# A decoder step in split fp32: convolution taps dealt differently, third output tile's weights first, last tile in column blocks

## What is computed

```
x = x + W_out [ conv_group(h) ; GLA_group(h) ],   h = RMSNorm(x), one projection W_in
x = x + CrossAttn(RMSNorm(x), memory K/V)         4 heads, 256 memory tokens
x = x + W_down relu(W_up RMSNorm(x))^2            4096 hidden
y = RMSNorm(x) * final_g
```

## Time and profile before

| | |
|---|---|
| median of three runs | 1539.58 us (1538.15 to 1540.58) |
| profiled execution | 1538.49 us |
| its span in the trace | 1536.8 us, granted PE clock 0.982 |
| PE busy | 1469.4 us, 96% |
| DVE, ACT, POOL busy | 611.8, 452.6, 383.5 us |
| DMA | 113.99 MB, mean 74 GB/s |

### The profile page before, as it was taken

The page is one execution under the profiler, slowest core; times in us unless marked ns, Lnnn a source line. Parts: engine busy times, 40 slices in busy tenths (PEclk is TensorE's granted clock), DMA queues, the critical chain, the costliest instruction groups (busy, mean ns, idle before and its releaser), DMA issues.

```text
span 1536.8 us, 22391 instructions
## 1 busy us (share of the span) xinstructions
PE 1469.4 (96%) x9454; PEld 1429.3 (93%) x9454; DVE 611.8 (40%) x681; ACT 452.6 (29%) x606; POOL 383.5 (25%) x292
## 2 busy tenths in 40 slices
PE   5799998998989999999999999999999999999994
PEld 5799997998779999988999999999999999999994
DVE  4759989995442355552322211112011110121213
ACT  6532252348252343341232211122012220032211
POOL 5753231122402311101222222222222222122220
PEclk9999999999889999999999999999999999999997
DMA  8411151011132241176111111111111111111102
GB/s 302 139 63 49 43 54 42 28 41 45 57 138 106 88 172 42 42 268 221 54 42 54 43 55 41 41 54 42 55 41 41 53 42 55 41 41 54 42 27 110
DMA packets 45273, 113.99 MB, mean 74 GB/s; under 512 B 7688, under 2 KB 20248, under 8 KB 43808
## 3 DMA queue, kind: packets, MB, share of 16 engines
q1 hardware_dynamic: 43312, 104.19, 20.6%
q10 hardware_dynamic: 1904, 8.98, 1.4%
HBM read 100.85 MB, written 12.30 MB: 74 GB/s over the span
## 4 chain that ended last, share of the span: by engine, by line
PE 83%; DVE 6%; issue 5%; ACT 3%; POOL 3%; DMA 0%; ACTq 0%; DVEq 0%; SPq 0%; POOLq 0%
PE ps L1080 57%; PE ps L1181 11%; PE ps L1433 5%; DVE ps L1644 2%; PE ps L1467 2%; PE m L1151 1%; POOL w_split L570 1%; PE ps L1386 1%; PE m L1346 1%; PE ps L1194 1%; PE ps L1446 1%; ACT w_split L633 1%; DVE x_res L2052 1%; PE m L1099 1%; POOL a_op L586 1%
## 5 line engine op out<-in xcount | busy, mean ns | idle before, releaser
L570 POOL TENSOR_TENSOR w_split<-w_raw,w_split 128x512 fp32r<-128x512 f32 x234 | 325.2, 1410 | 1094.1 <-ACT w_split L633 1094.0
L1080 PE MATMUL ps<-a_op,w_split 128*128 128x344 f32 x3312 | 524.0, 320 | 4.6 <-POOL w_split L570 4.6
L1080 PEld LDWEIGHTS ps<-a_op,w_split 128*128 128x128 f32 x3312 | 522.7, 189 | 5.0 <-DVE x_res L1845 4.8
L1080 PE MATMUL ps<-b_op,w_split 128*128 128x344 f32 x2304 | 362.6, 319 | 0.0
L1080 PEld LDWEIGHTS ps<-b_op,w_split 128*128 128x128 f32 x2304 | 361.7, 188 | 0.2
L1181 PE MATMUL ps<-a_op,w_split 128*128 128x344 f32 x1440 | 233.4, 321 | 0.0
L1181 PEld LDWEIGHTS ps<-a_op,w_split 128*128 128x128 f32 x1440 | 226.6, 188 | 1.9 <-issue 1.4
L633 ACT ACTIVATE w_split<-w_raw 128x1024 fp32r<-128x1024 f32 x117 | 122.8, 1050 | 243.4 <-PE ps L1080 238.6
L1644 DVE SCALAR_TENSOR_TENSOR ps<-conv_in,par,ps 128x1024 f32<-128x1024 f32 x116 | 149.7, 1290 | 3.7
L2023 DVE SCALAR_TENSOR_TENSOR tmp<-ps,rstd 128x1032 f32<-128x1032 f32 x32 | 39.4, 1233 | 215.1 <-PE ps L1080 203.2
L2033 DVE TENSOR_TENSOR x_res<-x_res,ps 128x1032 f32 x24 | 29.5, 1230 | 230.8 <-PE ps L1080 230.8
(11 more groups left out here) (206 smaller groups left out, 1046.4 us busy)
## 6 DMA issues: line engine op xcount, KB each, us to landing
w_raw<-in_wt SPq DMA_DIRECT2D x117, 512.0 KB, 3.5
cache_b<-in_cache_v SPq DMA_DIRECT2D x8, 1024.0 KB, 12.1
x_in<-in_x ACTq DMA_DIRECT2D x4, 1032.0 KB, 10.8
x_spill<-x_res SPq DMA_DIRECT2D x8, 516.0 KB, 2.6
out_y<-x_res ACTq DMA_DIRECT2D x8, 516.0 KB, 3.0
w_more<-in_wt SPq DMA_DIRECT2D x8, 512.0 KB, 4.0
cache_a<-in_cache_k SPq DMA_DIRECT2D x2, 2048.0 KB, 11.6
cache_b<-in_cache_k SPq DMA_DIRECT2D x2, 2048.0 KB, 11.5
```

The source lines that it names most:

```text
L570: gp.tensor_tensor(w_split[:, slot, 1, part, :], src, w_split[:, slot, 0, part, :].bitcast(F32), ALU.subtract).then_inc(w_low_done, 1)
L1080: last = pe.matmul(ps[:, b, 0:w], w_split[:, slot, wp, k, :], src[:, k, xp, c0:c0 + w], start=(k == 0 and j == 0), stop=(k == KT - 1 and j ...
```

## The change

Taps: after u_product of the last channel tile 26 instead of 24; before the units 10 instead of 16; behind the units 1, 5, 1, 5, 1, 5, 1, 6, 1, 7, 3. "mean" and "var" stand one block later among PE's slots, Ln and Exp likewise, the normalising multiplications behind unit 15, the swish between the key reads. Key turns and chunk sums are interleaved. The first two output tiles go over the GLA k-tiles in another order, and w_high of the third is called before their residuals. The last tile is made in column blocks of 392, 384 and 256. For each block the sum of squares is taken with the tokens on partitions (acc and the squares are the stationary operand, one column of ones moves), ACT takes a Sqrt of 128 x 2 to 4 numbers, DVE the reciprocal, and PE spreads them to all partitions by a product of the broadcast column with the identity; DVE scales from PSUM, and SP issues two stores of four k-tiles each.

```diff
+END_GROUPS = [[(0, NS)] + [(NS + P * i, P) for i in range(3)],
+              [(NS + P * i, P) for i in range(3, 6)],
+              [(NS + P * i, P) for i in range(6, 8)]]
...
-SLOTS.setdefault((PLACE["in", I_R + 2], 0), []).append(("mean",))
-SLOTS.setdefault((PLACE["in", I_R + 3], 0), []).append(("var",))
+SLOTS.setdefault((PLACE["in", I_R + 2], 1), []).append(("mean",))
+SLOTS.setdefault((PLACE["in", I_R + 3], 1), []).append(("var",))
...
+            for b, (c0, w) in enumerate(END_BLOCKS):
+                for k in (0, KT // 2):
+                    sp.wait_ge(y_ready, KT * b + k + KT // 2)
+                    sp.dma_start(o["y"][:, k:k + KT // 2, c0:c0 + w], x_res[:, k:k + KT // 2, c0:c0 + w]).then_inc(y_stored, 16)
...
-                    if (i, b) == (I_R + 3, 0):
+                    if (i, b) == (I_R + 3, 1):
                         act.wait_ge(var_ready, 1)
...
+            key_read(0)
+            key_read(1)
+            silu(0)
+            key_read(2)
+            silu(1)
+            key_read(3)
+            silu(2)
+            silu(3)
             act.wait_ge(tile_done, T_OUT)
-            conv_high(0)
-            conv_high(1)
-            for g in range(4):
-                read(("kt", g), ...)
-            conv_high(2)
-            conv_high(3)
+            for m in range(CT):
+                conv_high(m)
...
-                if t != T_XO:
+                if t not in (T_OUT, T_XO):
                     w_high(t + 2, (t + 2) % 2)
+            w_high(T_OUT + 2, T_OUT % 2)
             for m in range(KT):
                 residual_tile(T_OUT + m, m, G_XA, 24, 9)
...
+            for b, (c0, w) in enumerate(END_BLOCKS):
+                act.wait_ge(end_evicted, b + 1)
+                act.activation(tmp[:, 1, c0:c0 + w], x_res[:, KT - 1, c0:c0 + w], ACT.Square).then_inc(end_square, 1)
+                act.wait_ge(sums_ready, 10 + b + 1)
...
+                    act.activation(root[:, g0:g0 + n_], M[b % 2][:, 0:n_], ACT.Sqrt, bias=small[:, 128:129],
+                                   scale=1.0 / D).then_inc(root_ready, 1)
...
-            for g in range(4):
-                key_turn(g)
...
+            key_turn(0)
+            key_turn(1)
             pe.wait_ge(ps_free, T_OUT)
+            chunk_sum(0)
+            chunk_sum(1)
+            key_turn(2)
+            chunk_sum(2)
+            chunk_sum(3)
+            key_turn(3)
...
-            for k in range(CT, KT):
-                for t in (T_OUT, T_OUT + 1):
-                    tile_product(t, t % 2, a_op, ALL, wait_gla, range(k, k + 1))
+            for t, ks in ((T_OUT, range(CT, CT + 1)), (T_OUT + 1, range(CT, CT + 1)),
+                          (T_OUT, range(CT + 1, KT)), (T_OUT + 1, range(CT + 1, KT))):
+                tile_product(t, t % 2, a_op, ALL, wait_gla, ks)
...
+            def end_sum(b):
...
+                for j, (c0, w) in enumerate(END_GROUPS[b]):
+                    pe.matmul(M[b % 2][0:w, j:j + 1], acc[:, c0:c0 + w], ones[:, 0:1], start=True, stop=False)
+                    last = pe.matmul(M[b % 2][0:w, j:j + 1], tmp[:, 1, c0:c0 + w], ones[:, 0:1], start=False, stop=True)
...
+            def end_spread(b):
...
+                    last = pe.matmul(END_RSTD[:, b, o_:o_ + w], root[0:w, g:g + 1].broadcast_to([w, P]), ident[0:w, 0:w],
+                                     start=True, stop=True)
...
+            end_block(0, range(0, KT))
+            end_block(1, range(0, 3))
+            end_sum(0)
+            end_block(1, range(3, 6))
+            end_spread(0)
+            end_block(1, range(6, KT))
+            end_block(2, range(0, 5))
+            end_sum(1)
+            end_block(2, range(5, KT))
+            end_spread(1)
+            end_sum(2)
+            end_spread(2)
...
-                taps(16 if m < 3 else 24)
+                taps(16 if m < 3 else 26)
...
-            taps(16)
+            taps(10)
...
-                if u < 9:
-                    taps(5 if u % 2 else 1)
-                if u == 9:
-                    taps(7)
+                taps((1, 5, 1, 5, 1, 5, 1, 6, 1, 7, 3)[u] if u <= 10 else 0)
...
+            end_evict(0)
+            end_rstd(0)
+            end_scale(0, range(0, 2))
+            end_evict(1)
+            end_scale(0, range(2, 6))
+            end_rstd(1)
+            end_scale(0, range(6, KT))
+            end_evict(2)
+            end_scale(1, range(0, 5))
+            end_rstd(2)
+            end_scale(1, range(5, KT))
+            end_scale(2, range(0, KT))
```

More of the change, by code:

```diff
@@ L69 @@
 LAST_BLOCK = NB - 1
+END_GROUPS = [[(0, NS)] + [(NS + P * i, P) for i in range(3)],
+              [(NS + P * i, P) for i in range(3, 6)],
+              [(NS + P * i, P) for i in range(6, 8)]]
+END_BLOCKS = [(gs[0][0], gs[-1][0] + gs[-1][1] - gs[0][0]) for gs in END_GROUPS]
+END_FIRST = [0, 4, 7]
 SLOTS = {}
@@ L407, in even_odd @@
             return v[:, :, 0, :], v[:, :, 1, :]
+        END_BANK = PS[bank_of(N_T - 1)]
+        END_RSTD = PS[1 - (bank_of(N_T - 1))]
+        root = small[:, 0:9]
         go_bank = [[PS[1][:, 0, :], PS[1][:, 1, :]], [PS[1][:, 2, :], PS[0][:, 2, :]]]
@@ L867, in _, with key_read, silu @@
                         act.activation(ln_sum, ln_sum, ACT.Exp, scale=-0.5).then_inc(ln_scale_ready, 1)
[L868 to L872, removed]
+            def key_read(g):
+                read(("kt", g), lambda b: b[:, :].rearrange("p (c a n) -> p c a n", c=2, a=2), k_in[:, 2 * g:2 * g + 2, :, :])
+            def silu(m):
+                act.wait_ge(conv_normed, m + 1)
+                act.activation(conv_y[:, m, :], conv_y[:, m, :], ACT.Silu, bias=par[:, P_LNB + m:P_LNB + m + 1],
+                               scale=par[:, P_LNG + m:P_LNG + m + 1]).then_inc(conv_silu, 1)
             def conv_high(m):
@@ L1238, in _ @@
                     between(T_IN + i, b)
-            pe.wait_ge(k_updated, 14)
-            for g in range(4):
-                key_turn(g)
             def chunk_sum(c):
@@ L1541, in ffn_group @@
                         tile_product(g * 16 + i * 2 + (T_FF + j), (T_FF + j) % 2, b_op, ALL, no_wait, bank=bank_of(T_FF + j))
-                with pe.Fori(0, KT // 2) as i:
+                with pe.Fori(0, KT // 2 - rest) as i:
                     for j in range(2):
@@ L1550, in _, with end_block @@
             ffn_group(0, first=True)
-            with pe.Fori(1, FG) as g:
+            with pe.Fori(1, FG - 1) as g:
                 ffn_group(g)
-            sums(33, 10)
+            ffn_group(FG - 1, rest=1)
+            t = N_T - 1
+            tile_product(t - 1, (t - 1) % 2, a_op, ALL, no_wait, bank=bank_of(t - 1))
+            def end_block(b, ks):
+                c0, w = END_BLOCKS[b]
+                if b == 0 and ks[0] == 0:
+                    pe.wait_ge(ps_free, t - 1)
+                    pe.wait_ge(w_low_done, 2 * t + 2)
+                for k in ks:
+                    for j, (wp, xp) in enumerate(((0, 0), (0, 1), (1, 0))):
+                        last = pe.matmul(END_BANK[:, b, 0:w], w_split[:, t % 2, wp, k, :], a_op[:, k, xp, c0:c0 + w],
+                                         start=(k == 0 and j == 0), stop=(k == KT - 1 and j == 2))
+                if ks[-1] == KT - 1:
+                    last.then_inc(end_block_done, 1)
@@ new lines, in end_spread @@
+            def end_spread(b):
+                if b == 0:
+                    pe.wait_ge(ps_free, t)
+                pe.wait_ge(token_rstd, b + 1)
+                for j, (c0, w) in enumerate(END_GROUPS[b]):
+                    o_ = c0 - END_BLOCKS[b][0]
+                    g = END_FIRST[b] + j
+                    last = pe.matmul(END_RSTD[:, b, o_:o_ + w], root[0:w, g:g + 1].broadcast_to([w, P]), ident[0:w, 0:w],
+                                     start=True, stop=True)
+                last.then_inc(rstd_spread, 1)
```

64 lines of the change are left out of this document (46 added, 18 removed).

## The result

The changed kernel takes 1515.42 us (median of four runs, 1513.10 to 1516.91) where the kernel before took 1540.08 beside it (1538.15 to 1541.68): a ratio of 0.9844 [0.9831, 0.9856], 24.7 us faster. The forecast was 1516.6. The profiled execution took 1516.91 us with a span of 1515.2 and a granted PE clock of 0.990 (before 0.982).

The account below looks back on a forecast made before the run. PE, the matrix engine, was taken as the bound, with 83% of the chain; 9.8 + 7.2 + 6.0 = 23.0 us off the profiled 1538.49 gave 1515.5, and the median 1.1 above it 1516.6, range 1512.5 to 1525.

Parts of the forecast that it names:

- Sum A: Taps and layer norm, from the units to the sample state: 9.8 us earlier, ends 5 and 11.5.
- One sign of being wrong: At unit 12 or before the first states: PE idle above 2 us would show the prediction wrong.
- Sum B: Third output tile: PE's 4.57 us gap and 2.6 of fallen clock go, 7.2 us, ends 4.6 and 7.3.
- Sum C: The end, last tile in column blocks with norm, scaling and stores: 6.0 us earlier, ends 2 and 7.5.
- The norm does not give the taps back: Rival at units 11 and 12: the norm slips and gives the taps' gain back, Sum A becomes 5, 1521.4; chance 0.21.
- The clock in the end stage: Rival in the last tile: PE's clock falls to half, Sum C becomes 2.5, 1520.1 us; chance 0.16.
- the third rival: Last stores: short runs held to 56 GB/s make the kernel slower, 1576 us as a median; chance 0.03.
- the third tile's weights: Rival at the third output tile: its weights still wait, Sum B is 0, 1523.8 us; chance 0.05.

Follow-up runs that it names:

- plus_norm: The kernel before with only the change's taps, layer norm slots, swish, key turns and chunk sums: 1526.7 us, ratio 0.9921.
- after_again: The changed kernel, unedited, measured again on another chip: 1513.13 us, ratio 0.9834 against the kernel before.
- states_first: The changed kernel with DVE making the first two states after two of the four normalising multiplications, the others between the next states: 1509.43 us, ratio 0.9803.
- plus_out: The kernel before with only the new order of the two first output tiles and the third's early w_high: 1532.59 us, ratio 0.9952.
- end_sums_twice: The changed kernel with every one-column sum product of the last tile done twice: 1519.33 us, ratio 0.9868 against the kernel before.
- taps_late: The changed kernel with two taps moved back from the softplus wait to before the units: 1521.01 us, ratio 0.9878 against the kernel before.
- mean_early: The changed kernel with the mean's channel sum back in its old slot, before unit 12's column block: 1516.5 us, ratio 0.985.

## Why the prediction was right

**Sum A (predicted 9.8).** sample_out came 9.8 earlier in the profile, 11.2 in plus_norm, 11.3 in after_again: right in its mechanism, at the low side of what other executions give, so it is luck that this execution meets it to 0.1 us. Its steps, on the scale of before (2.9 us off the starts above): unit 1 out of the way 8.55 earlier (8.8 said); PE's wait at unit 12 was 0.22 where 0.5 to 1.5 was said, since POOL's pair (333.56 to 336.11) fell on the taps ahead of DVE's three sums, and each sum took 1.23; the key turns 1.47 behind unit 15 (1.5); the multiplications ended at 372.5 (372.6); the outputs at 378.2 (377.6). The clock fell in the 3.49 us and was 0.50 for the first outputs, for which 1.5 had been allowed: the chunk sums and the last key turn in front, slowed too, made the outputs 10.7 earlier instead of 11.3, and the first ten output products took 0.9 more, 1.5 together. In after_again, where the clock was back by 379, the outputs were 11.3 earlier and nothing was lost behind. POOL's sample state had 2.9 us to spare, not 3.6. One sign of being wrong that the prediction gave did appear, PE idle above 2 us before the first states (3.49). It contradicts the prediction's own sum, which has PE with little to do from 365 to 374 and the multiplications done only at 372.6; the sum was right and the sign badly chosen. The sum stood up because each late engine had been named, DVE's multiplications among them; what the prediction did not ask is whether their order was worth changing; states_first lies 6.0 us under the changed kernel's first median and 3.7 under its second.

**Sum B (7.2).** Met: 7.2 in the profile, 7.0 by plus_out's median (5.5 to 9.2). Both terms are borne out, 4.57 of gap and 2.6 of clock. The two halves of the step are not additive, each alone leaves under 2 us of gap.

**Sum C (6.0).** Undersized by 1.3. The term mis-sized is DVE's end, 24.9 us after the tile's start by the prediction, 23.8 measured. Its parts, predicted and measured: the first scaling begins at 10.7 and 10.4; the 24 scalings take 10.6 and 12.0; evictions and reciprocals 1.4 and 0.8; the wait for the second and third root 2 and 0.6. The four predicted parts add up to 24.7, so 0.2 is a slip of the sum. The scalings were taken too short against the prediction's own rows: 0.49 for 392 columns lies under the 0.514 that it quotes for 344, and a straight line through its two rows (0.514 for 344, 1.23 for 1032) gives 0.56, 0.56 and 0.42, 12.3 in all; 392 columns took 0.55. The wait was shorter because the one-column sums came every 0.22 us, not 0.30, and DVE had pieces of block 1 to do. So two errors of 1.4 cancelled, and the rest made the sum too small. The stores landed 4.1 behind DVE, 4.2 said.

**Together.** 24.3 by stages against 23.0, and the median 1515.42 against 1516.6. Sum C's 1.3 is as large as the 1.2 between the medians, but this does not identify it: two medians of the changed kernel differ by 2.3, and the second, 1513.13, is 3.5 under the forecast. The mechanism was right; that the first median came within 1.2 us is partly luck.

**The rivals.** The norm does not give the taps back: 0.22 us at unit 12. The clock in the end stage does not fall before the last spread, but end_sums_twice shows that it can and that it is one doubling of the sums away, at 5.4 us; it deserved its chance. The Trainium skill (TensorE: Matmul & The Clock Gate, What's actually happening) has throttling as the default state and activity as what lifts it. The trace agrees so far that the clock falls, to 0.50 behind the doubled sums and not behind the single ones (1.00); PE was busy by the profile in both, and no run here shows what counts as activity. The stores moved 355 GB/s where the third rival wanted 56. PE did not wait for the third tile's weights.

**Left open.** Why PE's first product of W_in, and with it unit 0, starts up to 4 us apart between executions. Part of sample_out ran at half clock in every profile, and it took 3.89 to 6.46 us. Whether real work there would hold the clock, and whether a smaller first block or some of the scaling on another engine would shorten the end: neither was tried.

## What to carry to other kernels

Price a wait of PE at its length plus what the clock does behind it: here 2.5 us more of idle time, in two waits close together, cost 5.6 (taps_late), while single waits of 1.3, 1.7 and 2.8 left the clock at 1.00 and cost only themselves (mean_early has the 2.8). The length of a wait alone does not tell it; look at the granted clock behind it. When a bulk pass and small results that PE waits for stand on one engine, put the small ones first as soon as their inputs are there: that gained 3.7 to 6.0 us on top of the change (states_first). Undo or add the parts of a change one by one and read distances from a common instruction, not absolute starts. Where a wait shrinks, see whether its releaser came sooner or the engine that waits came later: in mean_early it was the second.

## What the runs showed of the hardware that I had not expected

- **One-column products.** An fp32 product with one moving column starts every 0.22 us at full clock. PE is busy with them by the profile. The clock was 1.00 behind runs of eight and six of them in the changed kernel, and 0.50 for 3 us behind runs of sixteen and twelve in end_sums_twice.
- **The clock is not a property of the code alone.** The changed kernel, profiled twice, had the same waits and was at half clock to 382 in one and to 378 in the other; at the sample's outputs it fell 0.7 us into sample_out in one and 2.4 in the other. Together with the later start it makes 4.7 us, more than many of the edits.
- **Neighbours on POOL.** Four DVE multiplications of 1032 columns took 6.81 us with POOL's subtractions beside the first ones, 1.23 each alone (states_first, its last two). The two last taps, which read PSUM, took about 1.3 each with POOL's pair beside them.
- **Stores of short runs.** 1 to 1.6 KB per run moved 355 GB/s with the DMA engines full, where the former runs of 4128 bytes moved 413. The two differ also in the issuing queue and in how many k-tiles one store takes, so the length of the runs is not isolated.
